# Moving the input norm's per-token factor from the activations to the results of the input projections

## The chip, the cores and the metric

The kernel runs on one core of a Trainium2 chip. The metric is the device time of one execution in microseconds; smaller is better. All data is fp32.

## The reference, cut to what matters

```python
def rms_norm(x, w):
    y = x32 * lax.rsqrt(jnp.mean(x32 * x32, axis=-1, keepdims=True) + EPS)
    return y * w

xn = rms_norm(h, norm_mix_w[l])                 # (1024 tokens, 1024 features)
proj = jnp.einsum('bsd,de->bse', xn, w_in[l])   # 1024 x 8208
(da_q, da_k, da_v, ml_q, ml_k, ml_v, ml_i, ml_f, ml_o, gate_pre) = jnp.split(proj, ...)
# da_q, da_k: rotary embedding, differential attention, 8 heads
# ml_q, ml_k: causal convolution over 4 tokens plus bias, silu; ml_i, ml_f: exponential gates
# mLSTM in 8 heads; sigmoid(ml_o) gates its output; sigmoid(gate_pre) gates both branches
# then the branch projections, w_out, an FFN of width 4096 and a final norm
```

`rsqrt(mean(x*x)+EPS)` is one number per token. `norm_mix_w` is one number per feature, and the projection sums over the features.

## The kernel before, in words

Every matrix product is made from two-part numbers. ScalarE writes a rounded high part (`r1h` of the input, `w_hi` of a weight block), VectorE or GpSimd subtracts it from the value to give a low part (`r1l`, `w_lo`), and TensorE adds three products, hi by hi, lo by hi and hi by lo. A *unit* is one block of 128 output features by half of the 1024 tokens: 8 slices of the contraction, three matmuls each, 24 in all, into the bank `gp0` or `gp1`. The unit after next writes the same bank, so it waits (`gp_free`) until the unit's result was evicted to `ev` and from there stored to `proj_d` in DRAM.

**Start.** `x` comes transposed in two halves of 512 tokens (`xt0`, `xt1`), four transfers each. For the first half ScalarE squares each piece, VectorE adds pairs, TensorE sums them over the features (`x_sums_part`), ScalarE and VectorE make the inverse root, and TensorE spreads it over 128 partitions (`x_spread`). Then VectorE multiplies each slice of `xt` by root and norm weight, ScalarE writes `r1h`, VectorE `r1l`, and `first_half` issues, slice by slice, three matmuls for the mLSTM gates `i` and `f` and three for block 0. The roots of the second half come from squares of the untransposed rows of `x`.

**Head 0's blocks.** Units k = 2 to 11 follow. Beside them ScalarE and VectorE work on the gate rows (`prologue_step(2)`: `erow`, an Exp and an Ln), the sine and cosine tables and the rows `u_d` and `inter_d`. VectorE's `init_done` at the end of this lets SP load the first head's q and k.

**Head rounds.** In round h = 1 to 7, TensorE interleaves the 12 units of head h with the attention and mLSTM of head h-1, in 16 slots. `QUARTERS` says how many quarters of a unit stand at the head of each slot; `attend(h, s)` is the slot's part of the attention on every engine. In slot s, TensorE computes the scores of query block s-3, VectorE their minimum `nb` and ScalarE the exponentials, VectorE then combines both maps into `at` (`a_done`), which TensorE transposes in slot s+1 (`combined_transpose`). VectorE also does one tap of the convolution of `ckq` in each of the slots 3 to 6, each linked to the one before by a wait. Every queue runs in program order.

**Gate round.** The 24 first units of the branch gates (`GATE_UNITS_AT`, one or two in each slot) stand beside the attention of head 7; units 24 to 31 follow, then the branch projections (`front_unit`). ScalarE evicts these units. For an even unit it also splits the next weight block, whose low part GpSimd makes (`split_lo`). `low_done` and `block_low_done` are what a unit waits for.

Of the kernel before, what the change touches and what calls it, by code (L numbers as in the profile page):

```python
# [15 lines left out]
P = 128  # L16
# [7 lines left out]
D = 1024  # L24
# [93 lines left out]
TOKENS_ON = (5, 6, 7, 3)  # L118
X_LOADED = (16, 16, 16, 32, 64, 16, 16, 16)
# [56 lines left out]
def build(nc, x, x_rows, x_halves, positions, in_blocks, in_if, columns, da_lambda,  # L176
# [12 lines left out]
    with ExitStack() as ctx:  # L189
# [24 lines left out]
        rfin = sb("rfin", [P, TT])  # L214
        dd = sb("dd", [P, TT])
# [26 lines left out]
        with ExitStack() as sc:  # L242
            xt = [sb(f"xt{i}", [P, KT, HALF], F32, sc) for i in range(2)]
            xsq = [nc.alloc_sbuf_tensor_at(f"xsq{i}", [P, 2, HALF], F32, offset=home["pair"] + 4096 * i) for i in range(XC)]
            ss = sb("ss", [P, TT], F32, sc)
            rstd0 = sb("rstd0", [P, TT], F32, sc)
# [3 lines left out]
            lamt = sb("lamt", [P, 4 * DK], F32, sc)  # L250
            lams = sb("lams", [P, 4], F32, sc)
            irow = sb("irow", [NH, S], F32, sc)
            frow = sb("frow", [NH, S], F32, sc)
            erow = sb("erow", [NH, S], F32, sc)
            mrow = sb("mrow", [NH, S], F32, sc)
            brow = sb("brow", [NH, S], F32, sc)
# [5 lines left out]
        urow = erow  # L262


        with heads, ExitStack() as sc:
# [5 lines left out]
            vs = sb("vs", [P, TT, 2 * DV], F32R, sc)  # L271
            pr = sb("pr", [P, 2, S], F32, sc)
            at = sb("at", [P, S], F32, sc)
            at3 = sb("at3", [P, HALF], F32, sc)
            ath = sb("ath", [P, TT, P], F32R, sc)
# [10 lines left out]
            nd = sb("nd", [P, TT, VW], F32, sc)  # L286
# [126 lines left out]
        x_sq, x_pair, x_sums, x_std, x_rstd = (sem(n) for n in ("x_squared", "x_paired", "x_sums", "x_std", "x_rstd"))  # L413
        x_bc, x_scaled = sem("x_roots_spread"), sem("x_scaled")
# [39 lines left out]
        DVE_HEAD = 39  # L454
# [5 lines left out]
        def _(sp):  # L460
# [85 lines left out]
            for c in range(XC):  # L546
                x_load(0, c)
            sp.dma_start(ident[:], c_ident).then_inc(ident_in, 16)
            sp.dma_start(cols[:], columns).then_inc(cols_in, 16)
            wload_head(0, 0)  # L550
            sp.dma_start(wif[:].rearrange("p k n -> p (k n)"), in_if).then_inc(wif_in, 16)
            for c in range(XC):
                x_load(1, c)
            sp.wait_ge(x_sums, 1)
            for t in range(4, TT):
                sp.dma_start(xsq[t - 4][:].rearrange("p a n -> p (a n)"), x[0, t * P:(t + 1) * P, :]).then_inc(x_in[TOKENS_ON[t - 4]], 16)
# [3 lines left out]
            wload_head(0, 1)  # L560
            sp.dma_start(cosT[:].bitcast(I32), positions[0].partition_broadcast(P)).then_inc(c2_in, 16)
            sp.dma_start(inv[:], c_inv).then_inc(c2_in, 16)
# [151 lines left out]
            sp.wait_ge(gemm_done, 2 * N_PA)  # L714
            front_quarter_load(0, 2)
# [165 lines left out]
        def _(pe):  # L881
# [39 lines left out]
            def x_sums_part(c):  # L921

                pe.wait_ge(x_pair, c + 1)
                for t in range(4):
                    bank = sbank[:, 1 + t, :] if t < 3 else gp[1]
                    mm = pe.matmul(bank[:, 0:4], xsq[c][:, 0, t * P:(t + 1) * P], ones[:, 0:4],
                                   start=(c == 0), stop=(c == XC - 1))
                if c == XC - 1:
                    mm.then_inc(x_sums, 1)

            def x_spread(i):

                pe.wait_ge(x_rstd, i + 1)
                for t in range(4):
                    root = rstd0[:, 4 * i + t:4 * i + t + 1].broadcast_to([P, P])
                    mm = pe.matmul((tr, ob)[i][:, t * P:(t + 1) * P], root, ident[:], start=True, stop=True)
                mm.then_inc(x_bc, 1)

            def first_half(i):

                t = slice(i * HALF, (i + 1) * HALF)
                for k in range(KT):
                    if i == 0 and k == 6:
                        x_spread(1)
                    pe.wait_ge(x_lo, KT * i + k + 1)
                    if i == 0 and k == 0:
                        pe.wait_ge(wif_l, 1)
                    pe.matmul(sbank[:, i, :], wifh[:, k, :], r1h[:, k, t], start=(k == 0), stop=False)
                    pe.matmul(sbank[:, i, :], wifh[:, k, :], r1l[:, k, t], start=False, stop=False)
                    gates = pe.matmul(sbank[:, i, :], wifl[:, k, :], r1h[:, k, t], start=False, stop=(k == KT - 1))  # L950
                    if k == KT - 1:
                        gates.then_inc(pro_pe, 1)
                    if i == 0 and k == 0:
                        pe.wait_ge(w_split, 1)
                    pe.matmul(gp[i][:], wh[0][:, k, :], r1h[:, k, t], start=(k == 0), stop=False)
                    pe.matmul(gp[i][:], wh[0][:, k, :], r1l[:, k, t], start=False, stop=False)
                    mm = pe.matmul(gp[i][:], wl[0][:, k, :], r1h[:, k, t], start=False, stop=(k == KT - 1))
# [4 lines left out]
            for c in range(XC):  # L962
                x_sums_part(c)
            warm_up(1)
            pe.wait_ge(ident_in, 16)
            x_spread(0)
            warm_up(2)
# [10 lines left out]
            for k in range(2, 2 * HB):  # L978
                head_unit(0, k)
# [311 lines left out]
        def _(act):  # L1291
# [14 lines left out]
            def evac(n, half, pair=False):  # L1306
                wait(act, st[half], 16 * n)
                act.wait_ge(gemm_done, 2 * n + half + 1)
                if pair:
                    act.activation(ev[half][:].rearrange("p (a t n) -> p t a n", a=2, t=2),  # L1310
                                   gp[half][:].rearrange("p (t a n) -> p t a n", a=2, t=2), ACT.Copy).then_inc(gp_free, 1)
# [7 lines left out]
            act.activation(rstd0[:, 0:1], ones[:, 0:1], ACT.Sqrt)  # L1319

            def x_square(i, c):

                act.wait_ge(x_in[XC * i + c], 16)
                act.activation(xsq[c][:], xt[i][:, 2 * c:2 * c + 2, :], ACT.Square).then_inc(x_sq, 1)

            def token_square(t):

                act.wait_ge(x_in[TOKENS_ON[t - 4]], X_LOADED[TOKENS_ON[t - 4]])
                act.activation(xsq[t - 4][:], xsq[t - 4][:], ACT.Square,
                               accum_out=ss[:, t:t + 1]).then_inc(x_sq, 1)  # L1330

            for c in range(XC):
                x_square(0, c)
            split_hi(0, 0, 0)
            act.wait_ge(x_sums, 1)
            for to, sums in ((rstd0[:, 0:3], sbank[:, 1:4, 0]), (rstd0[:, 3:4], gp[1][:, 0:1])):
                act.activation(to, sums, ACT.Sqrt, bias=eps[:, 0:1], scale=1.0 / D).then_inc(x_std, 1)
            act.wait_ge(wif_in, 16)
            act.activation(wifh[:, :, 0:NH], wif[:, :, 0:NH], ACT.Copy).then_inc(wif_h, 1)
            act.activation(wifh[:, :, 32:32 + NH], wif[:, :, NH:2 * NH], ACT.Copy).then_inc(wif_h, 1)  # L1340
            for i in range(2):
                for k in range(KT):
                    act.wait_ge(x_scaled, KT * i + k + 1)
                    act.activation(r1h[:, k, i * HALF:(i + 1) * HALF], xt[i][:, k, :], ACT.Copy).then_inc(x_hi, 1)
                    if i == 0 and k < 4:
                        token_square(4 + k)
                    if i == 0 and k == 4:
                        act.wait_ge(x_sq, XC + 4)
                        act.activation(rstd0[:, 4:8], ss[:, 4:8], ACT.Sqrt, bias=eps[:, 0:1], scale=1.0 / D).then_inc(x_std, 1)
                    if i == 1 and k == 5:  # L1350
                        split_hi(1, 0, 1)

            def prologue_step(k):
                if k == 2:

                    act.wait_ge(pro_dve, 2)
# [14 lines left out]
                if k == 8:  # L1371

                    for i, tab in enumerate((sinT, cosT)):
                        act.wait_ge(pro_dve, 2 * i + 3)
# [6 lines left out]
            for k in range(2 * HB):  # L1381
                for b in {2: (2, 3), 6: (4,), 8: (5,), 10: (6,)}.get(k, ()):
                    head_split(0, b)
                evac(k // 2, k % 2, k // 2 in (2, 3))
                prologue_step(k)

            def attend(h, s, evac_units, splits=None, behind_k=None):
# [51 lines left out]
                if s == 7:  # L1439
                    act.wait_ge(conv_done, h + 1)  # L1440
                    act.activation(sg[:], kqs[:], ACT.Sigmoid).then_inc(sg_ready, 1)
                    act.wait_ge(o_in, 16 * h + 16)
# [28 lines left out]
            def head_round(h, att):  # L1471
                for s in range(SLOTS):
# [6 lines left out]
                    for k in ENDS_AT[s][:-1]:  # L1479
                        evac(h * HB + k // 2, k % 2, k // 2 in (2, 3))  # L1480

                    def evac_units():
                        for k in ENDS_AT[s][-1:]:
                            evac(h * HB + k // 2, k % 2, k // 2 in (2, 3))
# [8 lines left out]
            for s in range(SLOTS):  # L1493
# [1120 lines left out]
```

## Time and profile before

| | |
|---|---|
| median of 3 runs | 1867.22 us (1865.58 to 1867.6) |
| profiled execution | 1863.34 us, span 1861.6 us |
| TensorE busy | 1846.6 us (99%) |
| VectorE busy | 1282.8 us (69%) |
| ScalarE busy | 979.0 us (53%) |
| GpSimd busy | 324.5 us (17%) |

Busy time counts instructions that run; what a queue waits for is in the chain of waits. The profiled execution is 3.9 us below the median. "Idle before" behind a row of the timeline is the time in which the engine stood still ahead of it, and the arrow says what ended it.

### The profile page before, as it was taken

Reading aid. Unit: us, or ns where it says so; the run is one execution under the profiler, and the core shown is the slowest. Engines: PE = TensorE matmul, PEld = TensorE weight load, DVE = VectorE, ACT = ScalarE, POOL = GpSimd, SP = SyncE. Lnnn points to the kernel's source line nnn. Section 1 sums busy time; section 2 is a strip of 40 time slices with the busy share of each in tenths; the row PEclk is TensorE's granted clock in tenths of the full one; section 3 lists DMA queues with packets and bytes.
Section 4 is the critical chain, followed back from the end, with each engine's and each line's share of the span. In section 5 each row is a group of like instructions: output and inputs, shape, how many; then the busy total and the mean of one; then the engine's idle time right before and its main releaser. Section 6 shows DMA issues by size and latency. Waiting matters only on the chain.

```text
span 1861.6 us, 26825 instructions
## 1 busy us (share of the span) xinstructions
PE 1846.6 (99%) x9736; PEld 1584.7 (85%) x9736; DVE 1282.8 (69%) x1673; ACT 979.0 (53%) x1561; POOL 324.5 (17%) x190
## 2 busy tenths in 40 slices
PE   8999999999999999999999999999999999999998
PEld 6989898989898989888888887878888888888887
DVE  7675858586767667645326866787868778688774
ACT  5455655656565656445326553238676575333343
POOL 2202021211111121254421314520000000021002
PEclk9999999999999999999999999999999999999999
DMA  6351515151424242465467626647758677364412
GB/s 225 107 167 57 193 58 198 51 190 59 157 85 162 85 164 90 142 208 181 151 229 276 238 102 220 227 162 259 247 208 310 204 276 260 147 237 151 155 68 91
DMA packets 112020, 316.25 MB, mean 170 GB/s; under 512 B 11433, under 2 KB 28457, under 8 KB 98881
## 3 DMA queue, kind: packets, MB, share of 16 engines
q1 hardware_dynamic: 109632, 306.76, 47.1%
q10 hardware_dynamic: 2304, 8.39, 1.1%
q8 instruction: 52, 0.85, 0.2%
q14 instruction: 32, 0.25, 0.0%
HBM read 219.62 MB, written 95.49 MB: 169 GB/s over the span
## 4 chain that ended last, share of the span: by engine, by line
PE 95%; DVE 3%; issue 1%; ACT 0%; DMA 0%; POOL 0%; DVEq 0%; ACTq 0%; POOLq 0%
PE gp L894 9%; PE gp L892 9%; PE gp L893 9%; PE scores L1201 6%; PE scores L1203 6%; PE scores L1205 6%; PE gp L912 3%; PE gp L910 3%; PE gp L911 3%; PE gp L1201 2%; PE gp L1203 2%; PE gp L1205 2%; PE ob L1057 2%; PE scores L1010 2%; PE scores L1009 2%; PE ob L1058 2%
## 5 line engine op out<-in xcount | busy, mean ns | idle before, releaser
L892 PE MATMUL gp<-r1h,w_hi 128*128 128x512 f32 x752 | 296.9, 395 | 0.0
L894 PE MATMUL gp<-r1h,w_lo 128*128 128x512 f32 x752 | 293.8, 391 | 0.0
L893 PE MATMUL gp<-r1l,w_hi 128*128 128x512 f32 x752 | 293.0, 390 | 0.0
L1201 PE MATMUL scores<-fxh,fqh 128*128 128x512 f32 x512 | 199.8, 390 | 1.8 <-DVE fxl L2196 1.7
L1203 PE MATMUL scores<-fxl,fqh 128*128 128x512 f32 x512 | 199.2, 389 | 0.0
L1205 PE MATMUL scores<-fxh,fql 128*128 128x512 f32 x512 | 199.2, 389 | 0.0
L894 PEld LDWEIGHTS gp<-r1h,w_lo 128*128 128x128 f32 x752 | 141.2, 188 | 30.2
L892 PEld LDWEIGHTS gp<-r1h,w_hi 128*128 128x128 f32 x752 | 141.3, 188 | 27.8
L893 PEld LDWEIGHTS gp<-r1l,w_hi 128*128 128x128 f32 x752 | 141.4, 188 | 27.6
L2422 POOL TENSOR_TENSOR w_lo<-w_raw,w_hi 128x1024 fp32r<-128x1024 f32 x25 | 60.6, 2424 | 489.3 <-ACT w_hi L1304 467.1
L912 PE MATMUL gp<-w_hi_pair,r1l 128*128 128x256 f32 x512 | 144.8, 283 | 0.0
L910 PE MATMUL gp<-w_hi_pair,r1h 128*128 128x256 f32 x512 | 144.8, 283 | 0.0
L911 PE MATMUL gp<-w_lo_pair,r1h 128*128 128x256 f32 x512 | 144.8, 283 | 0.0
L1430 ACT ACTIVATE pr<-scores,nb 128x256 f32<-128x256 f32 (+7 forms) x128 | 94.2, 740 | 57.5 <-DVE nb L1923 56.8
L2203 DVE TENSOR_TENSOR fxl<-xraw,fxh 128x2048 fp32r<-128x2048 f32 x54 | 123.4, 2285 | 0.0
L1313 ACT ACTIVATE ev<-gp 128x512 f32<-128x512 f32 x96 | 56.9, 592 | 124.7 <-PE gp L894 94.6
L1619 ACT ACTIVATE fqh<-rq 128x2048 fp32r<-128x2048 f32 x32 | 61.3, 1914 | 105.3 <-DVE rq L2232 64.3
L1201 PEld LDWEIGHTS scores<-fxh,fqh 128*128 128x128 f32 x512 | 96.1, 188 | 22.7 <-DVE fxl L2196 2.2
L1203 PEld LDWEIGHTS scores<-fxl,fqh 128*128 128x128 f32 x512 | 96.1, 188 | 20.1 <-issue 0.2
L1205 PEld LDWEIGHTS scores<-fxh,fql 128*128 128x128 f32 x512 | 96.1, 188 | 20.0
L1631 ACT ACTIVATE fxh<-xraw 128x2048 fp32r<-128x2048 f32 x54 | 102.7, 1903 | 6.9 <-DMA xraw<-xo_d 6.9
L2207 DVE TENSOR_TENSOR fql<-rq,fqh 128x2048 fp32r<-128x2048 f32 x32 | 73.2, 2288 | 43.0 <-ACT fqh L1619 43.0
(423 smaller groups left out, 4569.0 us busy)
## 6 DMA issues: line engine op xcount, KB each, us to landing
xraw<-xo_d SPq DMA_DIRECT2D x62, 1024.0 KB, 5.0
w_raw<-in_in_blocks SPq DMA_DIRECT2D x64, 512.0 KB, 3.7
proj_d<-ev SPq DMA_DIRECT2D x128, 256.0 KB, 2.7
rq<-in_ff_quarters SPq DMA_DIRECT2D x32, 1024.0 KB, 8.2
xo_d<-res SPq DMA_DIRECT2D x78, 256.0 KB, 3.4
xo_d<-ring SPq DMA_DIRECT2D x60, 256.0 KB, 3.5
xo_d<-item SPq DMA_DIRECT2D x24, 256.0 KB, 2.6
pq<-in_sq_quarters SPq DMA_DIRECT2D x5, 1024.0 KB, 6.9
```

Source lines behind the costliest of these rows:

```text
L892: pe.matmul(gp[half][:], wh[slot][:, k, :], hi[:, k, t], start=(k == 0), stop=False)
L893: pe.matmul(gp[half][:], wh[slot][:, k, :], lo[:, k, t], start=False, stop=False)
L894: mm = pe.matmul(gp[half][:], wl[slot][:, k, :], hi[:, k, t], start=False, stop=(k == KT - 1))
L910: pe.matmul(to, r1h[:, kk, t], whp[:, kk].rearrange("p a n -> p (a n)"), start=(kk == 0), stop=False)
L911: pe.matmul(to, r1h[:, kk, t], wlp[:, kk].rearrange("p a n -> p (a n)"), start=False, stop=False)
L912: mm = pe.matmul(to, r1l[:, kk, t], whp[:, kk].rearrange("p a n -> p (a n)"), start=False, stop=(kk == KT - 1))
L1201: pe.matmul(bank, qh[s % 3][:, k, cols], xh[s % 3][:, k, :], start=first and k == 0, stop=False, skip_group_check=True)
L1203: pe.matmul(bank, qh[s % 3][:, k, cols], xl[s % 3][:, k, :], start=False, stop=False, skip_group_check=True)
L1205: mm = pe.matmul(bank, ql[s % 3][:, k, cols], xh[s % 3][:, k, :], start=False, stop=(k == UN - 1), skip_group_check=True)
L1430: act.activation(pr[:, c, 0:(i + 1) * P], sp_[:, c, 0:(i + 1) * P], ACT.Exp, bias=nb[:, c:c + 1], scale=-1.0, accum_out=rs[:, i, c:c + 1]) ...
L1631: act.activation(xh[s % 3][:], xraw[(s + 1) % 2][:], ACT.Copy).then_inc(p_hi, 1)
L2203: dve.tensor_tensor(xl[s % 3][:], xraw[(s + 1) % 2][:], xh[s % 3][:].bitcast(F32), ALU.subtract).then_inc(p_lo, 1)
```

## The change

The operand of the projections is now `x` times the norm's weight, without the token's root: ScalarE writes `r1h` with the weight as the scale, and VectorE makes `r1l` in one operation. So `x_sums_part`, the first `x_spread`s, the multiplication of `xt` and three of TensorE's warm-up products go. The root of all 8 token blocks comes from squares of the untransposed rows (8 loads instead of 4, 8 squares instead of 4 pieces and 4 rows), and is put on the results:

```diff
 # SP: order of the first loads; all 8 row blocks of x are loaded, four of them over xt0
+x_load(0, 0); cols; wif; x_load(0, 1); wload_head(0, 0); x_load(0, 2); x_load(0, 3); x_load(1, 0..3)
+wload_head(0, 1); ident; lamt; carry; last; cosT <- positions; inv; tokens 0..7 (4..7 wait for x_lo 8)
+mask; keep; wload_head(0, 2)
 # SP, ahead of the third quarter of the branch projections
 sp.wait_ge(gemm_done, 2 * N_PA)
+sp.wait_ge(gp_free, 2 * N_PA)

 # TensorE: warm_up(4), first_half(0), first_half(1); in each half the gate products of four slices, then
 # the block's of the same four; then
+for q in range(4):
+    head_unit(0, 2, q)
+    if q == 1:
+        x_spread()                      # both halves, 8 matmuls in the program

 # ScalarE, start
+x_high(0, k) as the pieces land, wif and block 0 split between them; x_high(1, k); split_hi(1, 0, 1)
+for t in range(TT):
+    token_square(t)
+act.activation(rstd[:], ss[:], ACT.Sqrt, ...)      # ahead of the first eviction
+spread_roots()                                     # roots <- tr, ob; behind the splits at k == 2
 # ScalarE, units 4 to 7 of every head (v blocks, tokens on the partitions)
-act.activation(ev, gp, ACT.Copy)
+act.activation(to[:, 0], by_token[:, 0], ACT.Copy, scale=rstd[:, 2 * pair:2 * pair + 1])
+act.activation(to[:, 1], by_token[:, 1], ACT.Copy, scale=rstd[:, 2 * pair + 1:2 * pair + 2])

 # VectorE, start: low part of block 0 (was GpSimd), sine table before the gate rows
-dve.tensor_scalar(irow[:, t], sbank[0:NH, i, :], gb[0:NH, 0:1], None, ALU.add)       # and frow
+dve.tensor_tensor(irow[:, t], sbank[0:NH, i, :], roots[0:NH, t], ALU.mult)           # and frow
+dve.tensor_scalar(irow[:], irow[:], gb[0:NH, 0:1], None, ALU.add)                    # and frow
 dve.wait_ge(pro_act, 7)
+pro.link(dve.tensor_tensor(cosT[:], cosT[:], roots[:], ALU.mult))
+pro.link(dve.tensor_tensor(sinT[:], sinT[:], roots[:], ALU.mult))
+dve.wait_ge(c2_in, 16 * 2)
 dve.wait_ge(uw_st, 32)
 dve.sem_inc(init_done, 2)

 # VectorE, every head: slot 3, ahead of the first tap, and behind the last tap in slot 6
 dve.wait_ge(kq_in, 16 * h + 16)
+chain.link(dve.tensor_tensor(ckq[:, CONV - 1:], ckq[:, CONV - 1:], roots[:], ALU.mult))
...
+dve.wait_ge(o_in, 16 * h + 16)
+dve.tensor_tensor(osig[:], osig[:], roots[:], ALU.mult).then_inc(o_scaled, 1)

 # Evictions of the 32 gate units: from ScalarE to VectorE
+def gate_evac(k):
+    n, half = N_GATE + k // 2, k % 2
+    dve.wait_ge(st[half], 16 * n)
+    dve.wait_ge(gemm_done, 2 * n + half + 1)
+    dve.tensor_tensor(ev[half][:], gp[half][:], roots[:, half * HALF:(half + 1) * HALF], ALU.mult).then_inc(gp_free, 1)
+for s in range(SLOTS):
+    for k in GATE_UNITS_AT[s]:
+        if k > 2:
+            gate_evac(k)                # units 0 to 2 stand inside slot 0
+    attend(NH - 1, s, lows=False)
+units 24, 25, 26 follow, 27 and 28 behind the two turn_late, 29 to 31 between the first front_q_lo and front_x_lo
```

`roots` and `rstd` take room that `irow`, `frow`, `mrow` and `brow` (now over `xt0`) and `nd` (now over `ath`) give up.

## Rows read from the trace of the kernel before

**Rows 1.** The waits of TensorE: line, releaser, us, times, longest.
```profile
PE scores L948 <- DVE r1l L1775: 2.7, 3, 1.6
PE scores L919 <- POOL wifl L2425: 2.6, 1, 2.6
```
**Rows 2.** Timeline of TensorE, start: start, us, engine, line, out<-in, shape, count.
```profile
2.64 5.39 PE L919 MATMUL scores<-yrow,ones 128*128 128x512 f32 x8 [2.64 <-POOL wifl L2425]
...
15.76 0.50 PE L948 MATMUL scores<-r1h,wifh 128*128 128x512 f32 x1 [0.61 <-DVE r1l L1775]
...
26.55 1.05 PE L936 MATMUL ob<-ident,rstd 128*128 128x128 f32 x8
27.36 0.47 PE L948 MATMUL scores<-r1h,wifh 128*128 128x512 f32 x1
...
42.28 0.39 PE L892 MATMUL gp<-r1h,w_hi 128*128 128x512 f32 x1
...
47.72 0.39 PE L892 MATMUL gp<-r1h,w_hi 128*128 128x512 f32 x1
```
**Rows 3.** Timeline of ScalarE, start.
```profile
4.72 1.06 ACT L1324 ACTIVATE xsq<-xt 128x1024 f32<-128x1024 f32 x1 [1.91 <-DMA xt<-in_x_halves]
...
8.47 1.06 ACT L1324 ACTIVATE xsq<-xt 128x1024 f32<-128x1024 f32 x1 [0.22 <-DMA xt<-in_x_halves]
...
34.73 0.63 ACT L1344 ACTIVATE r1h<-xt 128x512 fp32r<-128x512 f32 x1 [0.63 <-DVE xt L1793]
35.26 1.05 ACT L1296 ACTIVATE w_hi<-w_raw 128x1024 fp32r<-128x1024 f32 x1
```
**Rows 4.** Timeline of ScalarE beside units 2 and 3.
```profile
47.98 0.60 ACT L1313 ACTIVATE ev<-gp 128x512 f32<-128x512 f32 x1 [2.78 <-PE gp L894]
...
54.84 0.58 ACT L1313 ACTIVATE ev<-gp 128x512 f32<-128x512 f32 x1
```
**Rows 5.** Timeline of VectorE beside units 1 and 2.
```profile
44.98 2.83 DVE L1827 SCALAR_TENSOR_TENSOR erow<-frow 8x1024 f32<-8x1024 f32 x1
```
**Rows 6.** Timeline of GpSimd beside units 1 and 2.
```profile
44.33 6.33 POOL L2422 TENSOR_TENSOR w_lo_pair<-w_raw,w_hi_pair 128x1024 fp32r<-128x1024 f32 x2 [5.51 <-ACT w_hi_pair L1304]
```
**Rows 7.** Timeline of slots 3 to 5 in round 2.
```profile
314.99 1.22 DVE L1859 TENSOR_TENSOR w_lo_pair<-w_raw,w_hi_pair 128x1024 fp32r<-128x1024 f32 x1
316.12 0.81 DVE L1954 TENSOR_SCALAR kqs<-ckq,hc 128x1024 f32<-128x1024 f32 x1
...
317.06 0.29 DVE L1903 TENSOR_TENSOR atl<-tr,ath 128x128 fp32r<-128x128 f32 x1
...
319.44 0.48 DVE L1936 SCALAR_TENSOR_TENSOR at<-pr,cc 128x256 f32<-128x256 f32 x1
...
320.11 0.38 PE L1071 MATMUL tr<-ident,at 128*128 128x128 f32 x2
```
**Rows 8.** Timeline of the end of the gate round: ScalarE, TensorE, GpSimd.
```profile
932.51 1.06 ACT L1296 ACTIVATE w_hi<-w_raw 128x1024 fp32r<-128x1024 f32 x1 [0.49 <-PE gp L894]
...
937.68 0.60 ACT L1313 ACTIVATE ev<-gp 128x512 f32<-128x512 f32 x1 [3.62 <-PE gp L894]
```
```profile
942.86 0.60 PE L1105 MATMUL tr<-ident,nd 128*128 128x128 f32 x4
...
943.65 0.47 PE L892 MATMUL gp<-r1h,w_hi 128*128 128x512 f32 x1
```
```profile
933.65 2.40 POOL L2416 TENSOR_TENSOR w_lo<-w_raw,w_hi 128x1024 fp32r<-128x1024 f32 x1 [4.84 <-ACT w_hi L1296]
```
**Rows 9.** The mLSTM norm in round 1: VectorE, then ScalarE.
```profile
288.25 0.17 DVE L1992 SCALAR_TENSOR_TENSOR d<-nd 128x8 f32<-128x8 f32 x1 [2.83 <-ACT nd L1454]
...
290.73 0.17 DVE L2002 TENSOR_SCALAR d<-d 128x8 f32<-128x8 f32 x1
...
291.67 1.23 DVE L2006 TENSOR_TENSOR nd<-nd,rm 128x1024 f32<-128x1024 f32 x1
```
```profile
292.52 0.36 ACTq L1466 DMA_DIRECT2D oa_d<-at  x1
```

More of the change, by code:

```diff
@@ L919, in warm_up @@
                     pe.matmul(sbank[:, 0, :], ones[:], yrow[:, 0:HALF], start=True, stop=True)
[L921 to L937, printed above, removed]
+            def x_spread():
+                pe.wait_ge(x_rstd, 1)
+                pe.wait_ge(ident_in, 16)
+                for i in range(2):
+                    for t in range(4):
+                        root = rstd[:, 4 * i + t:4 * i + t + 1].broadcast_to([P, P])
+                        mm = pe.matmul((tr, ob)[i][:, t * P:(t + 1) * P], root, ident[:], start=True, stop=True)
+                    mm.then_inc(x_bc, 1)
@@ L939, in first_half @@
             def first_half(i):
                 t = slice(i * HALF, (i + 1) * HALF)
[L942 to L951, printed above, removed]
+                for part in range(2):
+                    ks = range(4 * part, 4 * part + 4)
+                    for k in ks:
+                        pe.wait_ge(x_lo, KT * i + k + 1)
+                        if i == 0 and k == 0:
+                            pe.wait_ge(wif_l, 1)
+                        pe.matmul(sbank[:, i, :], wifh[:, k, :], r1h[:, k, t], start=(k == 0), stop=False)
+                        pe.matmul(sbank[:, i, :], wifh[:, k, :], r1l[:, k, t], start=False, stop=False)
+                        gates = pe.matmul(sbank[:, i, :], wifl[:, k, :], r1h[:, k, t], start=False, stop=(k == KT - 1))
+                    if part:
@@ L952, in first_half @@
                         gates.then_inc(pro_pe, 1)
-                    if i == 0 and k == 0:
+                    if i == 0 and part == 0:
                         pe.wait_ge(w_split, 1)
-                    pe.matmul(gp[i][:], wh[0][:, k, :], r1h[:, k, t], start=(k == 0), stop=False)
-                    pe.matmul(gp[i][:], wh[0][:, k, :], r1l[:, k, t], start=False, stop=False)
-                    mm = pe.matmul(gp[i][:], wl[0][:, k, :], r1h[:, k, t], start=False, stop=(k == KT - 1))
+                    for k in ks:
+                        pe.matmul(gp[i][:], wh[0][:, k, :], r1h[:, k, t], start=(k == 0), stop=False)
+                        pe.matmul(gp[i][:], wh[0][:, k, :], r1l[:, k, t], start=False, stop=False)
+                        mm = pe.matmul(gp[i][:], wl[0][:, k, :], r1h[:, k, t], start=False, stop=(k == KT - 1))
@@ L1332, in _ @@
-            for c in range(XC):
[L1333 to L1351, printed above, removed]
+                if t >= XC:
+                    act.wait_ge(x_in[t - XC], X_LOADED[t - XC])
+                elif t < 3:
+                    act.wait_ge(x_in[TOKENS_ON[t]], X_LOADED[TOKENS_ON[t]])
+                else:
+                    act.wait_ge(tok_in, 16)
@@ new lines, in _, with spread_roots @@
+            act.wait_ge(x_in[XC], X_LOADED[XC])
+            for k in range(KT):
+                x_high(1, k)
+            act.wait_ge(w_split, 1)
+            split_hi(1, 0, 1)
+            for t in range(TT):
+                token_square(t)
+            act.wait_ge(x_sq, TT)
+            act.activation(rstd[:], ss[:], ACT.Sqrt, bias=eps[:, 0:1], scale=1.0 / D).then_inc(x_std, 3)
+            def spread_roots():
+                for i in range(2):
+                    act.wait_ge(x_bc, i + 1)
+                    act.activation(roots[:, i * HALF:(i + 1) * HALF], (tr, ob)[i][:], ACT.Copy).then_inc(roots_ready, 1)
@@ L1579, in _ @@
                     split_hi(n + 1, (n + 1) // 2, (n + 1) % 2)
-                for i in range(2):
-                    evac(n, i)
-                    if j == 15 and i == 0:
-                        front_x_hi(0)
-                if j == 14:
-                    front_q_hi(0)
+            front_q_hi(0)
+            front_x_hi(0)
             front_q_hi(1)
@@ L1821, in _ @@
             dve.tensor_reduce(lams[:, 0:2], lv[:, :, 0, :], AX_X, ALU.add).then_inc(pro_dve, 1)
+            table(sinT, cosT[:], 0.0)
+            dve.wait_ge(x_std, 3)
+            dve.reciprocal(rstd[:], rstd[:]).then_inc(x_rstd, 1)
             for i in range(2):
@@ L1892, in attend @@
                             weight_low(h + 1, 1)
+                        if not lows:
+                            gate_evac(0 if x_ is kraw else 1)
                     dve.wait_ge(qk_hi, 6 * h + 4)
@@ L2108, in _ @@
                 turn_late(second)
-            for s in range(2):
-                front_q_lo(s)
-                front_x_lo(s)
+                gate_evac(27 + second)
+            gate_evac(29)
+            front_q_lo(0)
+            gate_evac(30)
+            front_x_lo(0)
+            gate_evac(31)
+            front_q_lo(1)
+            front_x_lo(1)
             for s in range(FRONT):
```

169 lines of the change are left out of this document (87 added, 82 removed).

## The prediction

> **What bounds the kernel now.** I read the page's first part, then the waits of TensorE, then the timelines at the start, of one round of heads, and of the gate round. TensorE is busy for 1846.6 of 1861.6 us, so a microsecond is won only where TensorE stands still or works on something that goes, and lost wherever it is made to wait. Its waits are few and nearly all at the start: 2.7 us for `r1l`, 2.6 us ahead of its first matmul [rows 1]. Every other one in the list is under 2 us, and nothing here touches it. Read TensorE's start next: the warm-up products run from 2.64 to 8.03, the first product of the projections starts at 15.76, unit 2 starts at 42.28 [rows 2]. From there matmuls follow each other without a gap to the end: a unit takes 47.72 - 42.28 = 5.44 us, 0.227 us for a matmul [rows 2]. `first_half` has 96 matmuls, 21.8 us; 26.5 pass. So the start holds 7.7 us between warm-up and first product, and 4.7 us of gaps and spreading behind it. That is what the change can win. What it can lose stands in the rounds, where VectorE gets more work and TensorE has no gap to lend.
>
> **The change part by part.**
>
> *Start, won.* Removed for TensorE: the sums, the first spread and the wait for a scaled `xt`. ScalarE can write `r1h` as soon as a piece and `cols` are there. Pieces land 1.25 us apart from 4.7 on (four squares from 4.72 to 8.47, each waiting for its piece) [rows 3]. ScalarE's half slices cost 0.53 us apart, a weight split 1.05 [rows 3]; the first `r1l` is there at about 6.5, the gates' low part near 7. TensorE's first product then comes right behind the warm-up at 8.0. Block 0 is the fourth large load (7.6 with the small ones), its high part 8.7, its low part on VectorE 10.0 (1.22 us for such a subtraction [rows 7]); the gate products of four slices cover TensorE until 10.8. The second half of `x` is the eighth to ninth large load, 4.7 + 8 x 1.25 + 0.3 = 15.0, needed at 8.0 + 10.9 = 18.9. So `first_half` can run without a gap until 8.0 + 21.8 = 29.8.
>
> *Start, given back.* Unit 2 needs `gp0`, whose eviction now stands in ScalarE's queue behind 8 squares and the root. Their last row block is the 19th large load: 4.7 + 18 x 1.25 + 1 for the small ones = 28.2, or about a microsecond later if the broadcast of the positions is slow; I take 28.7. ScalarE alone would be there at 15.0 + 8 x 0.53 + 1.05 + 8 x 1.06 = 28.8. With the last square (1.06), the root (0.3) and the eviction (0.6, [rows 4]) unit 2 starts at 30.7 (bounds 29.8, with early loads, and 32.0). The spread, formerly in `first_half`, is now inside unit 2: 27.36 - 26.55 = 0.81 for each half [rows 2], 1.65 in all, on the path. Unit 3 starts at 30.7 + 5.44 + 1.65 = 37.8 instead of 47.72: **9.9 us won**, 10 rounded (8.6 to 10.8).
>
> *Is it kept until unit 11?* The next deadline is unit 5, which needs unit 3's eviction, and that stands behind `erow`'s Exp and Ln: 54.84 - 48.58 = 6.3 us of ScalarE [rows 4]. New: spread at 33.4, `roots` copied by 35.8, the row products and biases (six, 0.7 each as any half row of this size) until 39.4, `erow` 1.2 or, as now, 2.8 [rows 5]: 40.6 to 42.2. Plus 6.3 and the eviction, 0.6: 47.5 to 49.1. Unit 5 starts two units later, at 37.8 + 2 x 5.44 = 48.7 or a little after. I take no stall; the bound is 1.5.
> In the present trace `erow` takes 2.83 us while GpSimd's two subtractions run from 44.33 to 50.66 [rows 5, 6]. By the Trainium skill (SBUF — State Buffer, on the DVE and GpSimd shared port), a VectorE operation with two SBUF inputs and a GpSimd one lock each other out for the whole instruction; the row agrees. By that rule the table products and `osig`'s, two SBUF inputs each, would wait too where a split runs beside them and the scaled evictions, with one input in PSUM, would not; the sum is the same by the rule and by the rows.
>
> *Tables.* `cosT` and `sinT` cost 2 x 1.22 us ahead of `init_done`, 4.6 if one meets GpSimd. This moves the first head's loads; VectorE stands idle in slot 0 anyway, for ScalarE, which waits for TensorE. Hidden; without that cover it would cost what exceeds it, once: 0 to 1.5 us.
>
> *Every head, slot 3: lost.* This is the edit that decides. VectorE in round 2: subtraction 314.99, first tap 316.12 to 316.93, `atl` 317.06, then minimum, and `at` for query block 1 ends at 319.92; TensorE's transposition of it is at 320.11 [rows 7]. It depends on `a_done`, and 0.19 us separate them, some 0.05 to 0.1 of which a semaphore takes. The product of `ckq` (128x1024, two SBUF inputs, 1.22 us [rows 7]) is linked in front of the first tap, and all that follows is one chain: `at` ends 1.18 us later. TensorE then waits about 1.05, and a first matmul behind a wait has its weight load in the open, 0.1 more: 1.15 us. Rounds 1 to 7 all show this pattern, with a distance of 0.19 or less (rows 7 stand for seven). **7 x 1.15 = 8.1 us lost** (6.5 to 9.5; below it nothing, if the rest of the chain has slack that I do not see). Behind the stall TensorE is late too, so the other waits of slots 5 to 7 keep their distance. In the gate round, where whole units stand between slots, it is hidden.
>
> *Every head, slot 6 and the v blocks: nothing.* `osig`'s 1.22 us delay slot 7 by 0.2 to 0.7, whose `at` TensorE wants over 2 us later. The split eviction costs ScalarE 0.2 us, four times a head, ahead of idle time of a microsecond.
>
> *Gate round.* ScalarE loses 32 evictions, VectorE gains them at about 0.7 us (a whole row of twice the columns is 0.81 to 1.22 [rows 7]). Most are covered: VectorE waits for the same units anyway. One is not. In slot 14 VectorE now first evicts units 21 and 22, and unit 22 ends at 937.6 [rows 8]. Only then comes the norm of the mLSTM: 290.90 - 288.25 = 2.65 us to the variance, 4.65 to `nd` [rows 9]. From 938.45: variance 941.1, `nd` 943.1. TensorE wants `nd` at 942.86 [rows 8]: 0.3 us. Worse, ScalarE waits for that variance in its slot 13, ahead of the split of block 60, which was at 932.51 [rows 8]. From variance to the end of its output's DMA issue take 292.88 - 290.90 = 1.98 us [rows 9]; split 943.05 to 944.1, GpSimd 2.4 us [rows 8] until 946.6. Unit 24 was at 943.65 [rows 8]: 2.9 more. **3.2 us lost** (2 to 4.5; slot 9, where an eviction stands ahead of a low part that TensorE wants, may add 0.5). The wait of SP for `gp_free` is behind a store of the same unit: nothing.
>
> *Sum.* -9.9 + 8.1 + 3.2 = +1.4 on the profiled execution's 1863.34 us, 1864.7. That execution is 3.9 below the median, so against the median I lay the same difference on 1867.22: 1868.6, say 1868.5.
>
> **The rivals.** What a measurement here can tell from no change is 0.2%, 3.7 us: under 1863.5 is faster, over 1871.0 slower.
> (a) As above, near 1868.5: chance 0.45.
> (b) The product of `ckq` is hidden: TensorE's transposition is not what waits, or the chain is shortened elsewhere. For it: only 1.2 us in a round where VectorE is idle for a third of the time. Against it: that idle time lies in slots 8 to 15, and rows 7 show none. 1867.2 - 9.9 + 3.2 = 1860.5; chance 0.2. A mixed case, half a stall a head and an open start, gives 1863: 0.05.
> (c) The start gives back what it wins: the squares end late because the load queue is longer by four row blocks, and ScalarE's Exp and Ln come late behind the roots. The place is unit 2 and unit 5; from a last row block at 30.5 and an `erow` at 43.5 on, TensorE waits some 1.8 us at the one and 1.5 us at the other beyond (a). With 6.6 won it is 1867.2 - 6.6 + 8.1 + 3.2 = 1871.9: slower, chance 0.17.
> (d) More stalls of the kind of slot 5 or slot 14, because VectorE's queue has evictions ahead of the softmax: each 1 us a head is 7 us, 1873 to 1876. For it: VectorE has hardly an idle microsecond in slots 0 to 6. Against it: the distances that I found there are 0.2 us only once, 1 us or more else. Chance 0.13.
>
> **How the numbers follow.** The likeliest is (a), 1866 to 1871 by its own bounds. Range 1860.5 to 1873: it reaches to (b) and (c). Faster 0.23, slower 0.30, within 0.2% the rest, 0.47.
>
> **What would show it.** In the new trace: TensorE's first projection product near 8.0 and unit 3 near 38; a wait of TensorE at `combined_transpose` for VectorE's `at`, about 1 us, seven times; a gap ahead of unit 24 behind GpSimd's `w_lo`. No row of the first kind and I am wrong on the gain; no seven waits, and it is (b). Waits on `gp` evictions in units 2 to 5 are (c), a longer round without that one wait is (d).

## The result

The kernel after takes 1878.69 us (median of 6 runs, 1874.34 to 1881.86) against 1867.35 for the kernel before on the same chip: a ratio of 1.0066, 95% interval 1.0055 to 1.0076. It is slower by 11.3 us. Forecast were 1868.5 and a range up to 1873. The profiled execution has a span of 1877.3 us, 15.7 more than the one of before. That is 4.4 us more than the medians differ by, because the profiled execution of before is one of its fastest (1863.34 against a median of 1867.35).

The waits of TensorE in the kernel after: line, releaser, us in total, times, longest.
```profile
PE tr L1076 <- DVE at L1953: 7.2, 7, 1.1
PE gp L904 <- ACT ev L1320: 5.3, 2, 3.0
PE scores L931 <- POOL wifl L2455: 2.6, 1, 2.6
PE gp L904 <- POOL w_lo L2446: 2.3, 1, 2.3
PE gp L1168 <- DVE res L2190: 2.2, 1, 2.2
PE scores L1206 <- DVE fxl L2226: 1.7, 1, 1.7
PE ob L1062 <- DVE atl L1920: 0.9, 1, 0.9
PE tr L1110 <- DVE nd L2026: 0.3, 1, 0.3
```
Beside [rows 1], the wait for `r1l` is gone and five lines are new (`at`, `ev`, `w_lo`, `atl`, `nd`); the one for `res`, 1.6 us before, is longer. The first is the forecast one, seven times. The timeline of TensorE at the start, to be held against [rows 2]:
```profile
30.42 0.39 PE L962 MATMUL gp<-r1h,w_lo 128*128 128x512 f32 x1
33.80 0.47 PE L904 MATMUL gp<-r1h,w_hi 128*128 128x512 f32 x1 [2.99 <-ACT ev L1320]
...
34.83 0.63 PE L904 MATMUL gp<-r1h,w_hi 128*128 128x512 f32 x1
...
42.77 0.39 PE L904 MATMUL gp<-r1h,w_hi 128*128 128x512 f32 x1
```
The first product is at 7.89 us (15.76 before), but unit 2 comes 3.0 us behind the end of unit 1, and unit 3 starts at 42.77: only 4.95 us of the forecast 9.9 are won. Mind the row at 34.83: a matmul of 0.63 us instead of 0.39. The same stretch by windows (duration; busy share and count of TensorE, its weight loads, VectorE, ScalarE, GpSimd; granted TensorE clock; DMA share; GB/s):
```profile
33.00:34.00 1.00, 0.20 (x1) 0.23 (x2) 0.50 (x2) 0.88 (x3) 0.00 (x0) 1.00 0.54 217
34.00:35.00 1.00, 1.00 (x4) 0.76 (x4) 0.00 (x0) 0.88 (x2) 0.00 (x0) 0.62 0.55 213
35.00:36.00 1.00, 1.00 (x4) 0.81 (x3) 0.00 (x0) 0.95 (x2) 0.37 (x1) 0.50 0.97 367
36.00:37.00 1.00, 1.00 (x4) 0.71 (x4) 0.00 (x0) 0.66 (x1) 1.00 (x1) 0.50 0.04 14
37.00:38.00 1.00, 1.00 (x5) 0.82 (x4) 0.00 (x0) 0.00 (x0) 1.00 (x2) 0.67 0.00 0
38.00:39.00 1.00, 1.00 (x10) 0.95 (x9) 0.00 (x0) 0.00 (x0) 1.00 (x2) 1.00 0.00 0
```
Behind the wait the granted clock is 0.50, that is 1.2 instead of 2.4 GHz, for more than three microseconds; 0.38 + 0.5 + 0.5 + 0.33 = some 1.7 us of full-speed work is lost. Such a stretch is called a fall of the clock below. In the profiled execution of before, no window between the first and the last unit shows this. After, it comes four times, each behind a wait of 2.2 us or more: at 34, 112, 955 and 1167 us, 1.7 us each. The page's row of the clock in forty slices (9 in all of them) hides it; only windows of a microsecond show it. Other executions of before seem to have such stretches too: of those taken beside the experiments, the 14 of 1867 us or more have a mean granted clock of 0.997 or 0.996, the 12 under 1865 us one of 0.998 or 0.999, and 0.001 of the span is 1.9 us, about one stretch. That would be most of the 4.4 us; no trace of such an execution is there to show it.

How far TensorE stands behind the kernel before, read at the same instruction in both timelines: -4.95 us at unit 3; +4.07 in head 1 (a wait of 2.3 at 112.96 us, the clock behind it); +8.53 over the seven rounds, 1.22 a round; +5.80 in the gate round (0.86 in slot 9, 0.32 for `nd`, 2.34 ahead of unit 24, 1.7 for the clock, 0.6 in small shifts); +2.2 at the start of the w_out stage (a wait of 2.25 instead of 1.6, and the clock). The sum is +15.7. Here -4.95 is a gain; the rest is lost. The sum is one of two executions; the medians differ by 11.3.

### The profile page after: what moved, and what is told of

Read it like the earlier page. It is cut to its first block, busy times and chain, and to the rows that moved or that the text cites. A ratio compares the mean times of both kernels' runs of the same rounds, so it can differ in the third digit from the quotient of the medians.

```text
span 1877.3 us, 26794 instructions
## 1 busy us (share of the span) xinstructions
PE 1848.6 (98%) x9698; PEld 1585.2 (84%) x9698; DVE 1312.6 (70%) x1705; ACT 972.0 (52%) x1565; POOL 318.7 (17%) x189
## 4 chain that ended last, share of the span: by engine, by line
PE 85%; DVE 8%; issue 3%; ACT 2%; DMA 1%; SPq 1%; DVEq 0%; POOL 0%; ACTq 0%
PE gp L904 7%; PE gp L906 7%; PE gp L905 7%; PE scores L1206 6%; PE scores L1210 6%; PE scores L1208 6%; PE gp L922 3%; PE gp L924 3%; PE gp L923 3%; PE gp L1206 2%; PE gp L1210 2%; PE gp L1208 2%; PE ob L1062 2%; PE ob L1063 2%; PE scores L1015 2%
## 5 line engine op out<-in xcount | busy, mean ns | idle before, releaser
L923 PEld LDWEIGHTS gp<-w_lo_pair,r1h 128*128 128x128 f32 x512 | 97.4, 190 | 0.4
```

Of the source, the lines that this page charges most:

```text
L923: pe.matmul(to, r1h[:, kk, t], wlp[:, kk].rearrange("p a n -> p (a n)"), start=False, stop=False)
```

## The experiments

All are medians of four to eleven runs, taken with the kernel before on the same chip. The expectations counted from 1867.35 for before; beside the experiments it ran 0.6 to 2.6 us faster (1866.75 to 1864.76), so compare the distances to before. Two theories stood: each long wait costs itself and a slow clock behind it; or the waits and VectorE's added work are all, and the slow stretches chance.

**The kernel after once more**, unchanged.

> The kernel after, unchanged, on this chip beside the others: 1878 to 1879 if chips do not differ. Its trace shows the same waits; where a wait is 2.0 to 2.3 us, the clock may fall behind it in this execution and not in the other.

Measured 1876.25, ratio 1.0063 (1.0049 to 1.0077): 10.4 us above before, 11.3 the first time. The same kernel thus differs by 0.9 us from itself, and the interval of this ratio alone is 2.6 us to either side: a difference of one or two microseconds between two kernels cannot be told. In the profiled execution TensorE waits 3.6 us ahead of unit 2 and the clock falls behind it; it waits 1.9 us in head 1 and the clock does not fall. Its span is 3.7 us shorter than the one above, with two slow stretches instead of four.

**Without the product in slot 3.**
```
-                    chain.link(dve.tensor_tensor(ckq[:, CONV - 1:], ckq[:, CONV - 1:], roots[:], ALU.mult))
```


> The kernel after without the product of the convolution rows with the roots in slot 3 (this leaves that scaling out). Theory: the seven waits of TensorE for `at` are this one product; without it they go from 1.1 us each to under 0.3, and with them 8.4 us: 1870.3 against 1878.7. The four waits of over 2 us and the slow TensorE clock behind each stay. Rival: the waits come from VectorE's load as a whole (the table products, the product of `osig`, scaled evictions on ScalarE); then some 0.5 us a head stay and the kernel takes about 1874.

Measured 1868.77, ratio 1.0012 (1.0003 to 1.0021): 2.8 us above before, 7.6 to 8.5 won. The line `tr <- at` is gone from TensorE's waits. It is this product.

**Without the other scalings of a head.** The product of `osig` is taken out and the v blocks are evicted in one unscaled instruction.
```
-                        dve.tensor_tensor(osig[:], osig[:], roots[:], ALU.mult).then_inc(o_scaled, 1)
...
-                    act.activation(to[:, 0], by_token[:, 0], ACT.Copy, scale=rstd[:, 2 * pair:2 * pair + 1])
-                    act.activation(to[:, 1], by_token[:, 1], ACT.Copy, scale=rstd[:, 2 * pair + 1:2 * pair + 2]).then_inc(gp_free, 1)
+                    act.activation(to, by_token, ACT.Copy).then_inc(gp_free, 1)
```


> The kernel after without the product of `osig` and with the v blocks evicted by one unscaled instruction as before (both scalings are left out). Theory: both are hidden in every head; the seven waits of 1.1 us stay, and the time is that of the kernel after within 1 us. Rival: they lengthen VectorE's and ScalarE's chains in slots 0 to 7 and have their share in the 8.4 us; then each wait is shorter by 0.2 us or more, 1877 or less.

Measured 1874.85, ratio 1.0053 (1.0039 to 1.0067), against 1876.25 for the kernel after on that chip. The waits of TensorE have the seven of 1.1 us unchanged:
```profile
PE tr L1076 <- DVE at L1952: 7.5, 7, 1.1
```
So the rival's mechanism falls: these scalings have no share in the seven waits. The time does not decide, as 1.4 us between the medians cannot be told from nothing.

**The same work in other slots.** Nothing is left out; the product goes to slot 4, the taps to slots 5 and 6.
```
-                if s == 3:
+                if s == 4:
                     dve.wait_ge(kq_in, 16 * h + 16)
                     chain.link(dve.tensor_tensor(ckq[:, CONV - 1:], ckq[:, CONV - 1:], roots[:], ALU.mult))
...
-                if 3 <= s < 3 + CONV:
-                    j = CONV - 1 - (s - 3)
+                for j in {5: (3, 2), 6: (1, 0)}.get(s, ()):
```


> The kernel after, with all its work, but the product of the convolution rows in slot 4, two taps in slot 5 and two in slot 6, so that slot 3 holds none of them. VectorE does as much in a head as in the kernel after. Theory: only slot 3 has no time to lend; slots 4 to 6 have 1.0, 1.2 and 2.5 us between `at` and its transposition, and take 0, 0.8 and 1.3 us more. The seven waits go as in the run without the product: 1868.8 to 1870.5. Rival: VectorE's sum of work in slots 0 to 6 is the limit; the wait moves to slot 6 or 7 (0.5 us or more a head), 1873 to 1877.

Measured 1867.51, ratio 1.0006 (0.9997 to 1.0015): 0.8 above before, which cannot be told from the run without the product (2.8 above); the seven waits are gone. VectorE in slot 3 of round 2, and where the product went, beside [rows 7]:
```profile
312.21 1.22 DVE L1861 TENSOR_TENSOR w_lo_pair<-w_raw,w_hi_pair 128x1024 fp32r<-128x1024 f32 x1
314.21 0.29 DVE L1920 TENSOR_TENSOR atl<-tr,ath 128x128 fp32r<-128x128 f32 x1 [0.78 <-ACT ath L1426]
...
316.98 1.22 DVE L1965 TENSOR_TENSOR ckq<-ckq,roots 128x1024 f32<-128x1024 f32 x1
...
328.18 2.60 DVE L1972 SCALAR_TENSOR_TENSOR kqs<-ckq,hc,kqs 128x1024 f32<-128x1024 f32 x2
330.69 1.22 DVE L1976 TENSOR_TENSOR osig<-osig,roots 128x1024 f32<-128x1024 f32 x1
```
VectorE now has an idle 0.78 us ahead of `atl`, where it had none, and 3.7 us of work in a row in slot 6, for which nobody waits. The load is not what costs; the slot is.

**Eviction of unit 0 ahead of the last squares.** In ScalarE's queue:
```
             for t in range(TT):
+                if t == 4:
+                    evac(0, 0)
                 token_square(t)
...
-                evac(k // 2, k % 2, k - 4 if k // 2 in (2, 3) else None)
+                if k:
+                    evac(k // 2, k % 2, k - 4 if k // 2 in (2, 3) else None)
```


> The kernel after, with the eviction of unit 0 put ahead of the last four squares in ScalarE's queue. Theory: unit 2 then starts behind unit 1 without its wait of 3.0 us, the granted clock stays at full speed there, which gives 1.9 more, and unit 3 is at 38.2 instead of 42.8: 4.6 to 4.9 won, 1873.9. Rival: the slow clock behind the wait is not the wait's doing; 3.0 won, 1875.7. Second rival: VectorE's and ScalarE's work of the first head does not move with TensorE, and the gain is lost again at unit 5 or in head 1: under 1 won.

Measured 1872.22, ratio 1.0028 (1.0016 to 1.004): 6.3 above before, 4 to 5 us won. Unit 2 follows unit 1 without a gap, the clock stays at 1.00, the spread waits 0.5 us, and unit 3 is at 38.56 instead of 42.77. What held the eviction back, in ScalarE's timeline of the kernel after, beside [rows 3]:
```profile
21.48 1.05 ACT L1301 ACTIVATE w_hi<-w_raw 128x1024 fp32r<-128x1024 f32 x1
22.69 1.06 ACT L1336 ACTIVATE xsq<-xsq 128x1024 f32<-128x1024 f32 x1 [0.16 <-DMA xsq<-in_x]
23.65 0.18 ACT L1336 ACTIVATION_READ_ACCUMULATOR xsq<-xsq 128x1 f32 x1
23.97 1.06 ACT L1336 ACTIVATE xsq<-xsq 128x1024 f32<-128x1024 f32 x1
...
32.87 0.30 ACT L1362 ACTIVATE rstd<-ss,eps 128x8 f32<-128x8 f32 x1
33.08 1.30 ACT L1320 ACTIVATE ev<-gp 128x512 f32<-128x512 f32 x2
```
A square with a row sum costs 1.28 us, not 1.06: the accumulator is read by an instruction of its own. Eight of them are 1.8 us. The second half of `x` came at 16.55 instead of 15.0, 1.55 us more, and its eight half slices ran until 21.48, 0.62 us apart instead of 0.53, 0.7 more. The squares never waited for the load queue but once, for 0.16 us.

**Waits filled with products that nobody reads.**
```
+                    for _ in range(2):
+                        pe.matmul(sbank[:, 2, :], ones[:], yrow[:, 0:HALF], start=True, stop=True)
...
+                if k == 24:
+                    pe.matmul(sbank[:, 0, :], ident[:], roots[:, 0:HALF], start=True, stop=True)
```


> The kernel after, with products that nobody reads filling two of TensorE's waits: two of 512 columns ahead of unit 2 (2.7 of 3.0 us) and one ahead of unit 24 (1.3 of 2.3 us). The units start no sooner. Theory: a wait of over 2 us is followed by some 3.4 us at half the clock; filled, that goes, and 1.9 + 1.7 = 3.6 us are won: 1875.1. Rival: the slow stretches have another cause (load, power, chance): granted clock as before behind both places, 1878.7, or a little more for the added products.

Measured 1873.38, ratio 1.0041 (1.0027 to 1.0054): 7.4 above before, 3.0 to 3.9 won with no unit released sooner. Windows ahead of unit 2 and behind it:
```profile
32.00:33.00 1.00, 0.33 (x1) 0.00 (x0) 0.85 (x3) 0.91 (x4) 0.00 (x0) 1.00 0.96 381
33.00:34.00 1.00, 0.46 (x2) 0.45 (x3) 0.15 (x1) 0.88 (x2) 0.00 (x0) 1.00 0.47 188
34.00:35.00 1.00, 1.00 (x6) 0.79 (x5) 0.00 (x0) 0.88 (x2) 0.00 (x0) 1.00 0.69 262
```
Six matmuls in the third window where the kernel after has four. The fill was smaller than planned: waits of 1.2 us ahead of unit 2 and of 1.5 ahead of unit 24 are left, and no slow clock follows either. Unfilled, the wait ahead of unit 2 was 2.9 us or more in six profiled executions, and each of them has the slow clock. So here it follows from TensorE's standing still. One thing it does not settle: this trace has 2.46 us of wait in head 1, unfilled, and no slow clock behind it either.

**Eviction of unit 22 behind the variance** (gate round, slot 14):
```
+                    if k > 2 and k != 22:
                         gate_evac(k)
...
                     dve.tensor_scalar(d2[:], d2[:], 1.0 / DV, EPS, ALU.mult, ALU.add).then_inc(varm, 1)
+                    if not lows:
+                        gate_evac(22)
```


> The kernel after, with VectorE's eviction of unit 22 moved behind the variance of the mLSTM norm in slot 14 of the gate round. Theory: the waits for `nd` (0.3 us) and for block 60's `w_lo` (2.3 us) are the place of this eviction; both go, and where the granted clock falls behind the second, 1.6 more: 1878.7 - 2.6 = 1876.1 down to 1874.5. Rival: the variance is late because of the eviction of unit 21 or of VectorE's own chain; then 2 us or more of wait stay ahead of unit 24 and the time is 1878.

Measured 1872.54, ratio 1.0033 (1.002 to 1.0045): 5.8 above before, about 5 won, a little more than expected. Both waits are gone. The rows of VectorE and ScalarE in the kernel after show the chain that was forecast from [rows 8, 9]:
```profile
946.42 0.69 DVE L1884 TENSOR_TENSOR ev<-gp,roots 128x512 f32<-128x512 f32 x1 [4.75 <-PE gp L906]
...
949.85 0.17 DVE L2022 TENSOR_SCALAR d<-d 128x8 f32<-128x8 f32 x1
```
```profile
950.11 0.21 ACT L1480 ACTIVATE d<-d 128x8 f32<-128x8 f32 x1 [12.65 <-DVE d L2022]
...
951.97 1.06 ACT L1301 ACTIVATE w_hi<-w_raw 128x1024 fp32r<-128x1024 f32 x1 [0.49 <-PE gp L906]
```

**Table products behind the release of the first loads.**
```
-            pro.link(dve.tensor_tensor(cosT[:], cosT[:], roots[:], ALU.mult))
-            pro.link(dve.tensor_tensor(sinT[:], sinT[:], roots[:], ALU.mult))
             dve.wait_ge(c2_in, 16 * 2)
             dve.wait_ge(uw_st, 32)
             dve.sem_inc(init_done, 2)
+            pro.link(dve.tensor_tensor(cosT[:], cosT[:], roots[:], ALU.mult))
+            pro.link(dve.tensor_tensor(sinT[:], sinT[:], roots[:], ALU.mult))
```


> The kernel after, with the two products of the rotation tables behind the release of the first head's loads instead of in front of it. Theory: the wait of 2.3 us at 113 us (and the clock that falls behind it) starts with these products, which let SP issue the loads of head 0 and the store behind them 4.6 us later; it goes, 3.9 us with the slow stretch: 1874.8. Rival: the store is late because SP's queue itself is 5 us behind TensorE, which won them at the start; then the wait stays, at 1878.

Measured 1874.03, ratio 1.0045 (1.0031 to 1.0058): 7.3 above before, 3 to 4 won. The wait at 113 us is gone. VectorE, then SP, in the kernel after:
```profile
85.87 3.30 DVE L1850 TENSOR_TENSOR sinT<-sinT,roots 128x1024 f32<-128x1024 f32 x1
```
```profile
89.29 0.34 SPq L517 DMA_DIRECT2D kraw<-proj_d  x1
...
94.68 1.56 SPq L495 DMA_DIRECT2D proj_d<-ev  x2
```
Then ScalarE and TensorE:
```profile
102.48 0.60 ACT L1320 ACTIVATE ev<-gp 128x512 f32<-128x512 f32 x1 [4.68 <-DMA proj_d<-ev]
```
```profile
112.96 0.80 PE L904 MATMUL gp<-r1h,w_hi 128*128 128x512 f32 x1 [2.29 <-ACT ev L1320]
```
With the edit SP issues `kraw` at 85.02. Twelve loads stand between it and the store of block 5 (`kqs` and `sg` in four parts each, `qraw`, `pr`, `v`, a weight block). ScalarE's next eviction waited 4.68 us for that store, and with it stood everything of ScalarE's slot 0 of head 0, up to the eviction that TensorE waits for at 112.96.

**Waits of known length.** In the kernel before, ahead of units 25, 27, 29 and 31, TensorE waits for a fill by GpSimd; it runs through `cosT` and `sinT`, which nobody needs by then.
```
+                if k in (25, 27, 29, 31):
+                    pe.wait_ge(init_done, {25: 8, 27: 10, 29: 12, 31: 16}[k])
...
+                for width in {12: (800,), 13: (700, 700), 14: (950, 950), 15: (1000,) * 4}[j]:
+                    pool.wait_ge(init_done, 7 + held)
+                    pool.memset(spare[held % 2][:, 0:width], 0.0).then_inc(init_done, 1)
+                    held += 1
```


> The kernel before, with four waits of TensorE put between the last units of the gate round (ahead of units 25, 27, 29, 31), each for a fill by GpSimd of growing length: waits of about 1.1, 1.7, 2.2 and 4.4 us, 9.4 in all. Theory: the first two cost what they last; behind the last the granted clock falls to half, for 1.7 to 3 us more; behind the third it falls in some runs: 1866 + 9.4 + 2 to 5, 1877.4 to 1880.4. Rival: each costs only itself: 1875.4.

Measured 1877.12, ratio 1.0056 (1.0043 to 1.007), 10.4 above before. The waits were 0.88, 1.54, 1.96 and 4.01, 8.4 in all; the other 2.0 are near the 1.7 of the one fall of the clock that the trace has, behind the last:
```profile
976.00:977.00 1.00, 0.77 (x3) 0.67 (x4) 0.00 (x0) 0.00 (x0) 0.18 (x1) 1.00 1.04 403
...
991.00:992.00 1.00, 0.58 (x3) 0.49 (x4) 1.00 (x1) 0.00 (x0) 0.37 (x1) 1.00 0.08 29
992.00:993.00 1.00, 1.00 (x5) 0.84 (x4) 0.46 (x1) 0.00 (x0) 0.00 (x0) 0.86 0.00 0
993.00:994.00 1.00, 1.00 (x4) 0.74 (x3) 0.00 (x0) 0.00 (x0) 0.00 (x0) 0.50 0.00 0
```
**Longer ones.** The same with other widths:
```
+                for width in {12: (750, 750, 750), 13: (870, 870, 870), 14: (1000, 1000, 1000), 15: (850, 850, 850, 850)}[j]:
```


> The kernel before, with four waits of TensorE ahead of units 25, 27, 29, 31, now of about 2.3, 2.7, 3.0 and 3.4 us (11.4 in all). Theory: the longer the wait, the surer the fall of the clock behind it, 1.9 us each: with a fall behind all four 1885.5, behind two 1881.7. Rival: only the wait of 4.0 us was long enough, or it was the load behind it: 1877.9.

Measured 1883.05, ratio 1.0095 (1.008 to 1.0111), 17.2 above before. The waits were 2.40, 2.71, 3.02 and 3.52, 11.65 in all: 5.6 us remain, which would be some three falls of 1.7; the median run has no trace. The profiled execution, 1878.7 us, is the lowest of its kernel, and of these four waits only the last, of 3.52 us, has a fall behind it. The mean granted clock fits: 0.998 in it, 0.996 to 0.993 in the other three, which are 3 to 6.5 us longer.

**Four edits together**: unit 0's eviction, loads, taps, unit 22's eviction; first with a fifth, which puts the eviction of unit 14 behind slot 9's low part.

> The kernel after, all of its work, with the edits of four runs together (eviction of unit 0 ahead of the last squares; loads of the first head released ahead of the table products; taps in slots 5 and 6; eviction of unit 22 behind the variance) and a fifth: the eviction of unit 14 behind slot 9's low part, for the wait of 0.9 us there. Theory: what is left is the gain of the start, 9.5 us at unit 3, less up to 2 us at the start of the w_out stage: 1857.5 to 1859.5, faster than before by 0.4%. Rival: the edits meet (TensorE, 9.5 us earlier, finds other things late, at unit 5, in head 0 or in slots 8 to 11): 1861 or more.

Measured 1857.12, ratio 0.9953 (0.994 to 0.9967), 8.7 us faster than before.

> The kernel with the four edits together, without the fifth (the eviction of unit 14 is back ahead of the low part in slot 9). With the fifth, TensorE waited 0.7 us for the low part and 1.7 us for that eviction ahead of unit 16, 2.4 in all. Theory: it was put too late; without it there is one wait of 0.9 to 1.5 us in slot 9 and none ahead of unit 16, and the time is 0.9 to 1.5 us less: 1855.6 to 1856.2. Rival: the long `at` of 2.6 us beside GpSimd's split sets both; then no gain, 1857.

Measured 1856.71, ratio 0.9958 (0.9945 to 0.9972), 8.1 faster: no difference to the five that can be told, so neither theory nor rival is decided. The fifth edit bought nothing; its 2.4 us of waits against 1.5 without it are too little to be told here. Without it all waits of TensorE are these, and no window between the first and the last unit shows a slow clock:
```profile
PE scores L931 <- POOL wifl L2458: 2.6, 1, 2.6
PE scores L1206 <- DVE fxl L2229: 1.7, 1, 1.7
PE gp L1168 <- DVE res L2193: 1.6, 1, 1.6
PE ob L1062 <- DVE atl L1923: 1.5, 1, 1.5
```
Unit 3 is at 38.64, 9.1 us ahead of before, and about 8 are still there at the end. The idea of the change is worth nearly the 9.9 that was forecast for its start; the kernel after gave it away in the four places that the edits touch. One by one the four edits won 21.5 to 25 us against the kernel after, together 18.5 to 19.4; with an interval of 1.7 to 2.6 us to either side of each ratio, whether they overlap is not shown.

## Why the prediction was wrong

The terms, in its own order:

- *Start, won.* First product 8.0 forecast, 7.89 measured; the first half ended at 30.65 instead of 29.8. Right but for 0.9 us, which cost nothing.
- *Start, given back.* "Unit 2 starts at 30.7", upper bound 32.0; measured 33.8. The sum had the wrong path: it let the last row block (28.7) set the time, with one square behind it, and ScalarE's own queue, which by its figures was through at 28.8 + 0.3 + 0.6 = 29.7, came second. In the trace that queue sets it, with three sizes wrong: the squares, taken at 1.06 us each where each is 1.28 with its accumulator read (1.8), the arrival of the second half of `x` (1.55) and its half slices (0.7). The spread was right, 1.7 us. With the slow clock behind the wait unit 3 was at 42.77, not 37.8. That is 4.95 of the miss.
- *Kept until unit 11.* No stall at unit 5, as forecast.
- *Tables.* "Hidden; without that cover 0 to 1.5 us, once." It was priced as VectorE's time. But what it delays is SP's queue: `kraw`, twelve more loads and a store behind them, and ScalarE behind the store. It cost 4.07 us in the profiled execution (2.3 of wait, 1.7 of clock), 3 to 4 by the run without it. The text named the moved loads and did not follow them.
- *Slot 3.* 8.1 forecast (7 x 1.15), 8.53 in the traces (7 x 1.22), 7.6 to 8.5 by the run without it. Right in place, cause and size.
- *`osig` and v blocks.* Nothing, right.
- *Gate round.* 3.2 forecast, 5.8 measured: 0.32 for `nd` (0.3 forecast), 2.34 ahead of unit 24, which with it makes 2.7 (2.9 forecast; the sum added 0.3 to it, though the 2.9 is counted from unit 24's old start and holds it), 0.86 in slot 9 ("may add 0.5"), 0.6 in small shifts, and 1.7 for the clock, not priced.
- *w_out stage.* Not in the sum; "nothing here touches it" was said of all waits under 2 us. The wait there is 1.6 us in nine of the fourteen profiled executions of all kernels here and 2.2 in five, one of them a variant of the kernel before; where it is 2.2 the clock may fall too (three of the five). So it does not hang on the change alone; what sets it stays open.

In the profiled executions +1.4 was forecast and +15.7 came, 14.3 us more. The step that failed first is a cost put at nothing: each wait was added at its own length, without the slow stretch behind it. Four of those are 6.8 us. The second is the path of "Start, given back": unit 2 came 3.1 us later than forecast, by ScalarE's queue and not by the loads. The third is the tables, "hidden": 2.3 us of wait by way of SP's queue. The w_out stage (0.6), slot 9 (0.9), slot 3 (0.4) and small shifts make up the rest. Two of the four long waits stand in the forecast's sum (unit 2, unit 24), two do not. In mechanism the nearest rival was (c), the start gives back, with 6.6 won; 4.95 were won. Its place at unit 2 was right, its place at unit 5 was not, and its 1871.9 was too low as well. In time the nearest was (d), 1873 to 1876, but of its stalls only slot 9's 0.86 came.

## What to carry to other kernels

A wait of a TensorE that is otherwise never idle is to be priced at its length and, from about 2 us on, at a chance of some 1.7 us more for the slow clock behind it (13 of the 23 waits of 1.8 to 2.5 us here, all six from 3.2 us on); so cut long waits to short ones first, or fill them with products that nobody reads. VectorE is idle for almost a third of the time, and yet a product of a microsecond is free in one slot and costs its full length, once a head, in another: compare the distance from result to consumer slot by slot before placing it. A release flag that moves by some microseconds moves the whole queue behind it; follow the loads to the engine that waits for the last of them.

## What the runs showed of the hardware

The granted clock behind a single wait. The fourteen profiled executions of all kernels here have 33 waits of TensorE of 1.8 us or more behind its first product. Of the 23 between 1.8 and 2.5 us, 13 are followed by a stretch at 0.50; of the four from 2.7 to 3.1 us, two; of the six from 3.2 us on, all. No shorter one is, among them fourteen of 1.7 us ahead of the first stage of the feed-forward part. Behind the same wait of 2.34 us ahead of unit 24 the clock fell in the kernel after and did not in the one without `osig`'s product. A fall lasts some 3.4 us and costs some 1.7; twice, around the end of a wait of 3.6 us at the start, it lasted 6.8 us, of which about 2.8 us of work were lost behind the wait. One execution of the kernel before, with the longer waits added, also had a slow stretch with no long wait ahead of it, at 12.4 to 15.8 us, between the warm-up and the first product: ahead of it TensorE ran the `x_sums` products of four columns each. Its first product is at 16.80 instead of 15.76. Why the same wait falls once and not the next time stays open.

VectorE beside GpSimd. In slot 9 of the gate round, with GpSimd's weight split running (2.5 us), a part of `at` took 2.62 us:
```profile
880.62 2.52 POOL L2446 TENSOR_TENSOR w_lo<-w_raw,w_hi 128x1024 fp32r<-128x1024 f32 x1 [0.94 <-ACT w_hi L1301]
880.80 2.62 DVE L1958 SCALAR_TENSOR_TENSOR at<-pr,cc 128x256 f32<-128x256 f32 x1
883.34 0.68 DVE L1884 TENSOR_TENSOR ev<-gp,roots 128x512 f32<-128x512 f32 x1
884.16 0.29 DVE L1920 TENSOR_TENSOR atl<-tr,ath 128x128 fp32r<-128x128 f32 x1
```
In a round the same shape takes 0.48 us. The eviction and the `atl` of slot 9 stand right behind it, and `sinT`'s product above (3.30 instead of 1.23 us) is the same. By the Trainium skill (SBUF — State Buffer, on its two separate sides) such a pair of operations takes an exclusive lock for the whole instruction; the traces agree, and VectorE's 32 evictions, with one input in PSUM, took 677 to 692 ns each, those beside a GpSimd operation too.
